# Three kept gates (0, 3 and 6) instead of two, two of them finished ahead of the Q blocks, a lower stock of conv work, and other segments at the end

## The chip, the cores and the metric

The kernel runs on the 8 cores of one Trainium2 chip, each with its own part of the tokens and without talk between them. Every core holds 1024 prompt tokens (with 32 more ahead of them, for the causal windows) and 64 sample tokens, and reads all weights. The metric is the device time of the slowest core, in microseconds (us); a kernel's time is the median of its runs.

## What is computed

One layer of a decoder with three head groups, then a final RMSNorm:

```python
h = rmsnorm(x, norm_g)
u_a, gate_a, glu_val, glu_gate, gate_b, q, gate_c = split(h @ w_in)     # 76 blocks of 128 columns
o_a = pool_mix(u_a, windows 2/4/8/16, w_pool) * silu(gate_a)            # head group A: 12 blocks
a   = glu_val * sigmoid(glu_gate)
o_b = (silu(layernorm(depthwise_conv31(a))) @ w_pw) * silu(gate_b)      # head group B: 12 blocks
o_c = cross_attention(q, mem_k, mem_v) * silu(gate_c)                   # head group C: 8 blocks, 4 heads
y   = rmsnorm(x + concat(o_a, o_b, o_c) @ w_out, final_norm_g)          # 32 blocks of 128 columns
```

For the prompt, mem_k and mem_v come from rmsnorm(mem_prompt) and two more matrices; for the samples they are read from a cache. States of the pooling and of the conv are also written out.

## The kernel before, in words

All activations lie transposed: channels on the partitions, the core's tokens along the columns (W = 1088, or NT = 1120 with the halo). A *block* is 128 output channels; a matmul unit is 256 KB of bf16 weights, eight k chunks of 128, and four units make a block of the input projection. Weights come through a ring of nine tiles, filled from GpSimd's queue in the order of use (`fill`, L364).

**Start.** While x is loaded, partial sums of some blocks are formed over the k chunks that are there (`SETS`, L439); those of two gates of head group A cover three of their four units and wait in `HGA`. Then `second_halves` (L768) finishes blocks: V 1, Q 0, Q 1 and, last, the two gates with `ga_spill(0)` and `ga_spill(1)` (L1065), which join the last unit, multiply by 1/rms (`RB`), take the silu and write the gate to DRAM. Their tiles are then used again by the memory's norm: `MQ` takes the squares of the memory (`mem_group`, L830), four times a square on ScalarE and a sum on VectorE, until `mem_hilo` writes `PBT` and TensorE can sum it (`mem_sum`). Memory K and V follow, as steps that `slip` puts between the units of other blocks (16 units each for K and V, twice).

**Middle.** The loop at L1166 sets the order of blocks by hand-made costs (`S.t`, `S.when`): a gate and a V block of head group B (`gg_block`, `v_block`) are issued when `backlog() < TH` (the conv work that waits for VectorE, in us) and when `others` has given at least `PACE` = 1.7 blocks for each pair before; else the next block of `others` goes (Q, gates of C, gates of B, some of which are spilled to DRAM through the tile `XG`). Every V block gives VectorE one depthwise conv (39 pieces), whose pieces are put between its other work (`pump`). `v_mult(j)` needs the tile EA[j % 2], so conv j - 2 must be done (`flush_conv`). After the last conv the LayerNorm is applied (L1134, L1135, silu L1131), and twelve pointwise blocks follow (`pw_block`), while spilled gates come back.

**Head group A.** Four groups: three u blocks each, with running sums on VectorE, the load of w_pool, then three gate blocks (`ga_block`) with a small product (`mix`) for each. Gates 0 and 1 come from DRAM.

**End.** 26 blocks of w_out for all columns (L1396); columns from T2 on (the last two of five segments) are parked in DRAM as partial results. Then the last six blocks run segment by segment (`SEG`): 6 x 32 matmuls a segment, the sum of squares, 1/rms, scaling of all 32 blocks on VectorE and GpSimd, stores on SP's queue. Parked blocks are reloaded into an area that an earlier segment has left (`AREA`, `reload`, L1536). `LP` holds the last six blocks of a segment, `xq_load` fetches their x on ScalarE's queue.

Of the kernel before, what the change touches and what calls it, by code (L numbers as in the profile page):

```python
# [16 lines left out]
KC = 32  # L17
NT = 1120
W = 1088
NP_ = 1024  # L20
EPS = 1e-6
NRING = 9
UNITS_AT_ONCE = 2
PACE = 1.7
UNIT_US = 1.85
SLACK = 1.8
TH = 90.0
POOLW = (2, 4, 8, 16)
# [3 lines left out]

SEG = ((0, 176), (176, 432), (432, 688), (688, 920), (920, W))
AREA = (0, 1, 2, 1, 0)
KEPT = [[0, 1, 2, 3], [4, 5, 6, 7], [8, 9, 10, 11], [12, 13, 14, 15, 16, 17], [18, 19, 20, 21], [22, 23, 24, 25]]
# [139 lines left out]
def build_program(loads=None):  # L175
# [34 lines left out]
    with contextlib.ExitStack() as st:  # L210
# [217 lines left out]
        def esa_load(j, after=()):  # L428
# [339 lines left out]
        def second_halves():  # L768

            z, zb = proj(BLK_V + 1, 32, 2)  # L770
            ev, _, evb = esa(1)
            dve(lambda e: e.tensor_tensor(out=EA[1][:, 0:1056], in0=EA[1][:, 0:1056], in1=z[:, 0:1056], op=ALU.add), 1056,
                r=[EAb[1], zb], w=[EAb[1]])
            dve(lambda e: e.tensor_tensor(out=ev[:, :, 30:34], in0=STs[:, 0:64].rearrange("p (s r) -> p s r", s=16),
                                          in1=z[:, 1056:NT].rearrange("p (s r) -> p s r", s=16), op=ALU.add), 64,
                r=[STsb, zb], wa=[evb])
            gate_mult(1)
            gate_mult(0)
            gate_sig(1)
            gate_sig(0)  # L780
            z, zb = proj(BLK_Q, 0, 2)
            gate_mult(1)
            q_out(0, z, zb)
            v_mult(1, None, None)
            gate_mult(0)
            v_mult(0, None, None)

            push_sample(0)
            push_sample(1)
            push_prompt(0)  # L790
            push_prompt(1)
            q_scale(0)
            z, zb = proj(BLK_Q + 1, 0, 2)
            q_out(1, z, zb)
            assert conv_done[0] < 0
            q_scale(1)
            given.add(("q", 0))
            for i in range(2):

                ga_spill(i)  # L800
                for k, v in HGA[i][1][0].r.items():
                    S._put(MQb.r, k, v)

# [258 lines left out]

        NGA = 2

        def ga_spill(i):  # L1065
            if i < 2:
                t, tb = rest(BLK_GA + i, HGA[i], 3)
                gate(t, tb[0], t, *tb)
            else:
                z, zb = proj(BLK_GA + i, 0)  # L1070
                t, tb = XG, KSTb
                gate(z, zb, t, *tb)
            S.dma("sp", lambda e: e.dma_start(out=gsp_d[26 - i], in_=t), r=tb, w=[GSPA[i]], kb=544)

        def gb_spill(i):
# [122 lines left out]
        for dj in range(12):  # L1198
            pw_block(dj)
            if dj < 5:  # L1200
                g, gb = GB[dj]
                S.dma("sp", lambda e: e.dma_start(out=g[:, 0:W], in_=gsp_d[27 + dj]), r=[GSP[dj]], w=[gb], sembuf=gb, kb=544)
            if dj in (7, 9):

                i = (dj - 7) // 2
                g, gb = GB[2 * i]
                S.dma("sp", lambda e: e.dma_start(out=g[:, 0:W], in_=gsp_d[26 - i]), r=[GSPA[i]], w=[gb], sembuf=gb, kb=544)

# [63 lines left out]
        def ga_block(j):  # L1272
            if j < 2:
                return
            if j < NGA:
                drain()
                g, gb = gates_a[j % 2]
                S.dma("sp", lambda e: e.dma_start(out=g[:, 0:W], in_=gsp_d[26 - j]), r=[GSPA[j]], w=[gb], sembuf=gb, kb=544)
# [159 lines left out]
        LPb = [[[like(p[2], "LP") for _ in range(3 - i)] for p in l] for i, l in enumerate(LP)]  # L1438
        assert 3 * N[0] + T3 <= W and all(3 * N[i] <= W for i in (2, 4)) and all(2 * N[i] <= 512 for i in (1, 3)) and HTX + 512 <= KC * NT // 2
        assert all(N[i] <= N[AREA[i]] for i in (3, 4))  # L1440
        for k in range(2):
            for b in LPb[0][k]:
                for key, v in ST[k][1].r.items():
                    S._put(b.r, key, v)
# [51 lines left out]
        def seg_sum(si):  # L1496
# [17 lines left out]
            for gi, g in enumerate(KEPT[0:NQ]):  # L1514
                ap, bs = area(gi, si), AB[gi][AREA[si]]
# [178 lines left out]
```

How the kernel before makes its waits and increments, by code:

```python
    def _wait(self, eng, key, val):  # L71
        if self.known[eng].get(key, 0) >= val:
            return
        if key == "pe":
            assert val <= self.cnt[key], "wait for a TensorE count that nothing raises yet"
        self.known[eng][key] = val
        self.h[eng].wait_ge(self.sems[key], val)
# [43 lines left out]
    def op(self, eng, fn, r=(), w=(), wa=(), inc=True, cost=0.1):  # L121
        ww = tuple(w) + tuple(wa)
        self.deps(eng, r, ww)
        end = self.when(eng, r, ww) + cost
        self.t[eng] = end
        for b in r:
            b.tr = max(b.tr, end + 0.1)
        for b in ww:
            b.tw = end + 0.1
            b.we = eng
        sem = self._sem(eng)
        ins = fn(self.h[eng])
        if inc:
            self.cnt[eng] += 1
            ins.then_inc(sem, 1)
            val = self.cnt[eng]
        else:
            assert eng == "pe"
            val = self.cnt[eng] + 1
        self._mark(eng, val, r, w, wa)
# [1 line left out]
    def dma(self, eng, fn, r=(), w=(), wa=(), sembuf=None, kb=None, beside=()):  # L142
# [7 lines left out]
            for b in ww:  # L150
                b.tw = self.tq + 1.0
                b.we = None
        sb = sembuf or (w[0] if w else r[0])
        if sb.dsem is None:
            sb.dsem = {}
        kind = "sw" if eng == "pool" else "hw"
        key = sb.dsem.setdefault(kind, ("dma", sb.name, id(sb), kind))
        sem = self._sem(key)
        self.cnt[key] += 16
        fn(self.h[eng]).then_inc(sem, 16)
        self._mark(key, self.cnt[key], r, w, tuple(wa) + tuple(beside))
```

## Time and profile before

| | us |
|---|---|
| median of 3 runs | 1841.94 (1841.41 to 1940.04) |
| the profiled execution | 1841.41 |
| its span on the slowest core, core 3 | 1840.3 |
| spans of the other cores | 1833.5 to 1839.4 |
| TensorE busy | 1790.8 (97%) |
| VectorE busy | 1057.7 (57%) |
| ScalarE, GpSimd busy | 375.9, 358.6 |

"Busy" of an engine is the time in which at least one of its instructions runs; matmuls overlap, so the mean of one is longer than the distance to the next. In the views, PE is TensorE, DVE VectorE, ACT ScalarE, POOL GpSimd, SP the queue of SyncE; `out<-in` are the program's tiles and L the line of the kernel. "[1.41 <-DVE Y L1566]" says that the engine stood idle for 1.41 us before the instruction, and what ended that. The granted clock is the share of TensorE's full clock that the chip let through: 1.00 is 2.4 GHz, 0.50 is 1.2 GHz.

### The profile page before, as it was taken

How to read it: one execution, taken by the hardware profiler on the slowest of the kernel's cores; microseconds unless marked ns; L12 is line 12 of the kernel's file. 1: busy time of each engine (PE TensorE's matmuls, PEld its weight loads, DVE VectorE, ACT ScalarE, POOL GpSimd, SP SyncE). 2: the span in 40 equal slices, each digit the busy share in tenths (PEclk: the TensorE clock that was granted, in tenths of full speed). 3: DMA queues.
4: the chain of work that ended last, by engine and by line, in shares of the span. 5: the costliest groups of instructions: out<-in, count | busy, mean ns of one | idle time of the engine just before them, and what ended most of it. 6: DMA issues, size and time to landing. Idle time of an engine off the chain costs nothing.

```text
span 1840.3 us, 31577 instructions; the slowest of 8 cores (1833.5 to 1840.3 us)
## 1 busy us (share of the span) xinstructions
PE 1790.8 (97%) x12286; PEld 927.3 (50%) x12286; DVE 1057.7 (57%) x1173; ACT 375.9 (20%) x599; POOL 358.6 (19%) x644
## 2 busy tenths in 40 slices
PE   6999999999999999999999999999999999999995
PEld 3444445555444555555444444444444444444695
DVE  3577997999899999998731332324311111212266
ACT  4534213112110211311410000000012222222211
POOL 2211221222222122212111111111111111111034
PEclk9999999999999999999999999999999999999998
DMA  9988788877999687777467656555657888766589
GB/s 237 245 187 178 110 131 129 139 110 115 136 167 151 103 117 124 117 108 112 66 125 112 95 80 85 76 85 79 107 98 136 140 142 138 140 121 127 92 244 312
DMA packets 126147, 244.57 MB, mean 133 GB/s; under 512 B 17072, under 2 KB 34736, under 8 KB 123440
## 3 DMA queue, kind: packets, MB, share of 16 engines
q0 software_dynamic: 87840, 168.79, 62.2%
q1 hardware_dynamic: 18864, 58.50, 10.1%
q10 hardware_dynamic: 19296, 15.26, 2.9%
q8 instruction: 99, 1.62, 0.4%
q14 instruction: 48, 0.39, 0.1%
HBM read 360.56 MB, written 34.63 MB: 215 GB/s over the span
## 4 chain that ended last, share of the span: by engine, by line
PE 88%; DMA 4%; issue 3%; DVE 3%; ACT 1%; POOL 0%; ACTq 0%; DVEq 0%; POOLq 0%; SPq 0%
PE Z L312 82%; PE PM L312 6%; DMA CC<-xT 2%; DMA ring<-w_in 1%; DVE KEEP L832 1%; DMA mkN<-KEEP 0%; DMA yT<-CC 0%; DMA KV<-w_pool 0%; ACT CC L546 0%; DVE CC L420 0%; POOL HT L1519 0%; PE PM L941 0%; ACT CC L831 0%; DVE CC L808 0%; DMA yT<-QS 0%
## 5 line engine op out<-in xcount | busy, mean ns | idle before, releaser
L312 PE MATMUL Z<-HT,ring 128*128 128x512 bf16 (+3 forms) x7184 | 1147.2, 319 | 21.2 <-DMA ring<-w_in 16.2
L312 PEld LDWEIGHTS Z<-HT,ring 128*128 128x128 bf16 x7184 | 555.3, 98 | 589.0 <-issue 29.7
L312 PE MATMUL Z<-CC,ring 128*128 128x512 bf16 (+5 forms) x3288 | 484.9, 311 | 0.2 <-DVE KEEP L970 0.2
L312 PEld LDWEIGHTS Z<-CC,ring 128*128 128x128 bf16 x3288 | 250.6, 98 | 233.1 <-issue 0.4
L373 POOL DMA_DIRECT2D ring<-w_in x304 | 161.9, 534 | 671.9 <-PE Z L312 387.9
L706 DVE SCALAR_TENSOR_TENSOR CC<-EA,CS,CC 128x1024 f32<-128x1024 f32 x180 | 230.0, 1278 | 0.0
L710 DVE SCALAR_TENSOR_TENSOR Y<-EA,CS,Y 128x1024 f32<-128x1024 f32 x168 | 214.7, 1278 | 0.0
L1409 DVE TENSOR_TENSOR HT<-Z,EA 128x256 f32<-128x256 f32 (+1 forms) x54 | 18.1, 391 | 199.4 <-PE Z L312 199.4
L373 POOL DMA_DIRECT2D ring<-w_out x113 | 59.6, 528 | 353.4 <-PE Z L312 334.0
L971 ACT ACTIVATE KEEP<-KEEP 128x1088 f32<-128x1088 f32 x21 | 23.3, 1111 | 215.4 <-DVE KEEP L970 215.3
L1239 DVE TENSOR_TENSOR EA<-Z,KEEP 128x1040 f32<-128x1040 f32 x12 | 14.9, 1242 | 87.6 <-PE Z L312 87.6
L312 PE MATMUL PM<-ring,CC 128*128 128x512 bf16 x256 | 59.7, 379 | 2.3 <-ACT KV L890 2.3
L1411 ACT ACTIVATE SG<-HT 128x256 f32<-128x256 f32 (+1 forms) x51 | 20.1, 395 | 188.4 <-DVE HT L1409 185.1
L1409 DVE TENSOR_TENSOR KEEP<-Z,EA 128x256 f32<-128x256 f32 (+1 forms) x24 | 8.0, 391 | 87.4 <-PE Z L312 87.4
L971 ACT ACTIVATE SG<-SG 128x1088 f32<-128x1088 f32 x6 | 6.7, 1111 | 252.1 <-DVE SG L970 252.1
L1414 DVE TENSOR_TENSOR SS<-SS,SG 128x1088 f32<-128x1088 f32 x25 | 32.3, 1292 | 26.7 <-ACT SG L1411 26.7
L1519 POOL TENSOR_TENSOR HT<-HT,SS 128x512 f32<-128x512 f32 (+3 forms) x30 | 33.4, 1145 | 69.5 <-DVE SS L1513 69.5
L970 DVE TENSOR_TENSOR KEEP<-Z,KEEP 128x1088 f32<-128x1088 f32 x20 | 25.7, 1287 | 33.3 <-PE Z L312 30.5
L1295 DVE SCALAR_TENSOR_TENSOR CC<-PM,CS,SG 128x512 bf16<-128x512 f32 (+1 forms) x18 | 10.7, 595 | 56.1 <-PE PM L312 55.4
L312 PEld LDWEIGHTS PM<-ring,CC 128*128 128x128 bf16 x256 | 23.4, 98 | 29.5 <-issue 2.6
L420 DVE TENSOR_TENSOR CC<-CC 128x2240 f32<-128x2240 f32 x15 | 37.3, 2486 | 0.2 <-DVE CC L420 0.2
L734 ACT ACT_TABLE_LOAD x9 | 11.5, 1283 | 119.4 <-DVE KEEP L733 88.5
(234 smaller groups left out, 1218.6 us busy)
## 6 DMA issues: line engine op xcount, KB each, us to landing
ring<-w_in POOLq DMA_DIRECT2D x304, 256.0 KB, 5.7
ring<-w_out POOLq DMA_DIRECT2D x113, 256.0 KB, 4.2
CC<-xT POOLq DMA_DIRECT2D x14, 1120.0 KB, 15.9
EA<-xT SPq DMA_DIRECT2D x26, 544.0 KB, 6.0
ring<-w_mem_k POOLq DMA_DIRECT2D x32, 256.0 KB, 6.7
ring<-w_mem_v POOLq DMA_DIRECT2D x32, 256.0 KB, 6.5
ring<-ckT POOLq DMA_DIRECT2D x32, 256.0 KB, 5.1
ring<-cvP POOLq DMA_DIRECT2D x32, 256.0 KB, 5.0
```

The source lines that it names most:

```text
L312: S.op("pe", lambda e: e.matmul(out, lhsT=lhsT, rhs=rhs, start=start, stop=stop, skip_group_check=skip), r=r, w=w, inc=inc, cost=max(0.026 ...
L373: S.dma("pool", lambda e: e.dma_start(out=RING[s][:, 0:n], in_=src), r=after, w=[RINGb[s]])
L420: dve(lambda e: e.tensor_tensor(out=ACC, in0=ACC, in1=SQ2[a % 2], op=ALU.add), 2240, r=[ACCb, SQ2b[a % 2]], w=[ACCb])
L706: piece(lambda e, k=k: e.scalar_tensor_tensor(out=YB[j][:, 0:NP_], in0=EA[b][:, 2 + k:2 + k + NP_], scalar=col(wc + k), in1=YB[j][:, 0:NP_ ...
L710: piece(lambda e, k=k: e.scalar_tensor_tensor(out=Y1[:, 0:NP_], in0=EA[b][:, 2 + k:2 + k + NP_], scalar=col(wc + k), in1=Y1[:, 0:NP_], op0 ...
L832: piece(lambda e: e.tensor_reduce(out=MA[:, g, :], in_=MQ.rearrange("p (k n) -> p n k", k=8), axis=AX.X, op=ALU.add), 3300, r=[MQb], wa=[M ...
L970: dve(lambda e: e.tensor_tensor(out=g[:, 0:W], in0=z[:, 0:W], in1=RB[:, 32:NT], op=ALU.mult), W, r=[zb, RBb], w=gb)
L971: act(lambda e: e.activation(out=g[:, 0:W], in_=g[:, 0:W], func=AF.Silu), W, r=gb, w=gb, tab="silu")
L1409: dve(lambda e: e.tensor_tensor(out=yv, in0=z[:, c0:c1], in1=xr[:, c0:c1], op=ALU.add), c1 - c0, r=[zb, xrb], w=[yb])
L1411: act(lambda e: e.activation(out=sq[:, c0:c1], in_=yv, func=AF.Square), c1 - c0, r=[yb], **({"wa": [sqb]} if i else {"w": [sqb]}))
L1414: dve(lambda e: e.tensor_tensor(out=SY[:], in0=SY[:], in1=SQo[:, 0:W], op=ALU.add), W, r=[SYb, SQob], w=[SYb])
L1519: S.op("pool", lambda e: e.tensor_tensor(out=yv, in0=yv, in1=over(SY[:, c0:c1], 2), op=ALU.mult), r=[SYs[si], b], w=[b], cost=0.3 + n * 0. ...
```

## The change

- **Which gates.** Of head group A, gates 0, 3 and 6 go through DRAM (before: 0 and 1). Gates 0 and 3 have three units done at the start; gate 6 is a whole block of `others`, after the gates of C. `ga_block` computes the other nine. Gate 0 is reloaded during the pointwise blocks, gates 3 and 6 after the first u block of groups 1 and 2.
- **When.** In `second_halves` the two gates are finished ahead of the Q halves: the first behind the sigmoids, the second when the first conv pieces have been queued. `ga_early` also carries the planned reading time of the spilled tiles over to `MQ`.
- **Stock.** `TH` 90 to 62.
- **Segments.** Widths 176, 256, 256, 232, 168 to 224, 256, 224, 224, 160. The parked columns become 384 (before 400). Segment 3 uses the area of segment 0 and segment 4 that of segment 1 (before the other way round). The reload of segment 3 goes behind the stores of segment 0, that of segment 4 in three pairs between the stores of segment 2 (before: of 4 behind 0, of 3 behind 1). The last six blocks' tiles no longer overlap the staging tiles.

```diff
+NGA = 3
-TH = 90.0
+TH = 62
-SEG = ((0, 176), (176, 432), (432, 688), (688, 920), (920, W))
-AREA = (0, 1, 2, 1, 0)
+SEG = ((0, 224), (224, 480), (480, 704), (704, 928), (928, W))
-                (((BLK_GA, NSEG), (BLK_GA + 1, NSEG)), 0, 12),
+                (((BLK_GA, NSEG), (BLK_GA + 3, NSEG)), 0, 12),
 def second_halves():
             gate_sig(1)
             gate_sig(0)
-            z, zb = proj(BLK_Q, 0, 2)
+            ga_early(0)
             gate_mult(1)
-            q_out(0, z, zb)
             v_mult(1, None, None)
             gate_mult(0)
             v_mult(0, None, None)
...
             push_prompt(0)
             push_prompt(1)
+            ga_early(1)
+            z, zb = proj(BLK_Q, 0, 2)
+            q_out(0, z, zb)
             q_scale(0)
             z, zb = proj(BLK_Q + 1, 0, 2)
             q_out(1, z, zb)
...
-            for i in range(2):
-                ga_spill(i)
-                for k, v in HGA[i][1][0].r.items():
-                    S._put(MQb.r, k, v)
+        def ga_early(i):
+            ga_spill(i)
+            b = HGA[i][1][0]
+            for k, v in b.r.items():
+                S._put(MQb.r, k, v)
+            MQb.tr = max(MQb.tr, b.tr)
...
-        NGA = 2
         def ga_spill(i):
             if i < 2:
-                t, tb = rest(BLK_GA + i, HGA[i], 3)
+                t, tb = rest(BLK_GA + 3 * i, HGA[i], 3)
...
+        def ga_back(i):
+            g, gb = GB[2 * (i % 2)]
+            S.dma("sp", lambda e: e.dma_start(out=g[:, 0:W], in_=gsp_d[26 - i]), r=[GSPA[i]], w=[gb], sembuf=gb, kb=544)
...
-            if dj in (7, 9):
+            if dj == 7:
+                ga_back(0)
...
         def ga_block(j):
-            if j < 2:
-                return
...
+            if j in (0, 3, 6)[0:NGA]:
                 return
...
                 u_block(3 * g + i)
+                if i == 0 and 0 < g < NGA:
+                    ga_back(g)
...
-            if final and si < 2:
-                reload(4 - si, (3, 0, 4, 1, 5, 2))
+            if si == 0 and final:
+                reload(3, (3, 0, 4, 1, 5, 2))
+            if si == 2:
+                reload(4, {NFULL + 3: (3, 0), KEPT[3][0]: (4, 1), KEPT[4][0]: (5, 2)}.get(dbs[0], ()))
```

## Rows read from the trace of the kernel before

**Rows 1.** The page, busy time of the engines: us, share of the span, instructions.

```profile
PE 1790.8 (97%) x12286; PEld 927.3 (50%) x12286; DVE 1057.7 (57%) x1173; ACT 375.9 (20%) x599; POOL 358.6 (19%) x644
```

**Rows 2.** Waits of TensorE, core 3: what for, us in total, times, longest.

```profile
PE Z L312 <- DVE ESA L749: 4.4, 1, 4.4
...
PE PM L312 <- DVE PBT L846: 2.5, 1, 2.5
PE PM L312 <- ACT KV L890: 2.3, 1, 2.3
PE Z L312 <- DVE Y L1566: 1.4, 1, 1.4
PE PM L312 <- DVE CC L1295: 0.9, 1, 0.9
PE PM L312 <- DMA KV<-w_pool: 0.7, 1, 0.7
```

**Rows 3.** Spans and mean granted clock of the two slowest cores.

```profile
core 2: 1839.4 us, clock 0.993
core 3: 1840.3 us, clock 0.993
```

**Rows 4.** Waits of TensorE, core 2.

```profile
PE Z L312 <- DVE ESA L749: 4.8, 1, 4.8
PE PM L312 <- DVE PBT L846: 3.1, 1, 3.1
...
PE PM L312 <- DVE SS L1571: 2.1, 1, 2.1
```

**Rows 5.** Timeline (start us, us, instruction), the matmul behind the last segment.

```profile
1822.18 0.52 PE L312 MATMUL PM<-SS,SG 128*128 128x168 f32 x2 [3.15 <-DVE SS L1571]
```

**Rows 6.** Stretch of the last stage: us, busy us of PE, PEld, DVE, ACT, POOL, clock, DMA share, GB/s.

```profile
1757.00:1823.00 66.00, 62.63 (x654) 59.00 (x652) 46.93 (x93) 10.47 (x27) 22.93 (x19) 1.00 0.98 296
```

**Rows 7.** Timeline of VectorE and ScalarE around the early gates.

```profile
132.07 1.32 DVE L596 TENSOR_TENSOR SG<-SG,KEEP 128x1120 f32<-128x1120 f32 x1
...
151.67 1.28 DVE L808 TENSOR_TENSOR CC<-CC,Z 128x1088 f32<-128x1088 f32 x1
...
162.43 1.91 ACT L831 ACTIVATE CC<-CC 128x2048 f32<-128x2048 f32 x1 [6.88 <-DMA yT<-CC]
```

**Rows 8.** Stretches after the waits for PBT and L749, columns as in rows 6.

```profile
195.20:198.60 3.40, 3.40 (x15) 1.40 (x15) 3.40 (x4) 2.31 (x2) 0.00 (x0) 0.53 0.31 57
235.90:242.70 6.80, 5.12 (x17) 2.02 (x18) 6.63 (x9) 3.13 (x4) 0.00 (x0) 0.50 0.96 160
```

**Rows 9.** Timeline of TensorE and VectorE, V block 2 and conv 0.

```profile
211.61 3.62 PE L312 MATMUL PM<-ring,CC 128*128 128x512 bf16 x16
...
225.89 3.85 PE L312 MATMUL Z<-HT,ring 128*128 128x512 bf16 x24
...
235.41 0.73 DVE L725 COPY SS<-CC 128x1088 f32<-128x1088 f32 x1
...
237.57 13.76 PE L312 MATMUL Z<-HT,ring 128*128 128x512 bf16 x72 [4.38 <-DVE ESA L749]
```

**Rows 10.** Timeline of TensorE, two blocks of segment 0.

```profile
1738.35 5.01 PE L312 MATMUL Z<-CC,HT 128*128 128x176 bf16 x64 [1.41 <-DVE Y L1566]
```

**Rows 11.** Timeline of VectorE, first block of segment 4.

```profile
1809.94 0.33 DVE L1566 TENSOR_TENSOR Y<-Z,EA 128x168 f32<-128x168 f32 x1 [2.43 <-DMA yT<-Y]
```

**Rows 12.** DMA issues, 1823 to 1840 us: number, KB each, median us to landing.

```profile
yT<-HT ACTq DMA_DIRECT2D x3, 336.0 KB, 6.7
```

**Rows 13.** DMA issues, 1750 to 1757.5 us.

```profile
yT<-Y SPq DMA_DIRECT2D x1, 264.0 KB, 3.1
```

**Rows 14.** Timeline from V block 11 to the first pointwise block.

```profile
794.71 0.22 DVE L749 TENSOR_TENSOR ESA<-Z,KEEP 128x64 f32<-128x64 f32 x1
...
929.76 1.29 ACT L1131 ACTIVATE CC<-CC,CS 128x1088 bf16<-128x1088 f32 x1 [1.30 <-DVE CC L1135]
931.26 28.95 PE L312 MATMUL Z<-CC,ring 128*128 128x512 bf16 x187
```

More of the change, by code:

```diff
@@ L1061, in build_program @@
         gsp_d = y_d.rearrange("(b p w) -> b p w", b=32, p=128)
-        NGA = 2
         def ga_spill(i):
             if i < 2:
-                t, tb = rest(BLK_GA + i, HGA[i], 3)
+                t, tb = rest(BLK_GA + 3 * i, HGA[i], 3)
                 gate(t, tb[0], t, *tb)
             else:
-                z, zb = proj(BLK_GA + i, 0)
+                z, zb = proj(BLK_GA + 3 * i, 0)
                 t, tb = XG, KSTb
@@ L1202, in build_program @@
                 S.dma("sp", lambda e: e.dma_start(out=g[:, 0:W], in_=gsp_d[27 + dj]), r=[GSP[dj]], w=[gb], sembuf=gb, kb=544)
-            if dj in (7, 9):
-                i = (dj - 7) // 2
-                g, gb = GB[2 * i]
-                S.dma("sp", lambda e: e.dma_start(out=g[:, 0:W], in_=gsp_d[26 - i]), r=[GSPA[i]], w=[gb], sembuf=gb, kb=544)
+            if dj == 7:
+                ga_back(0)
         EU = EA
@@ L1215, in build_program @@
         gates_a = [(SG[0], SGb[0]), (G[0], Gb[0])]
+        assert gates_a[0] == GB[0] and gates_a[1] == GB[2]
         SPB = [Buf("SPL%d" % i) for i in range(3)]
@@ L1272, in ga_block @@
         def ga_block(j):
-            if j < 2:
-                return
[L1275 to L1278, printed above, removed]
+            if j in (0, 3, 6)[0:NGA]:
                 return
@@ L1348, in area @@
             m = len(KEPT[gi])
-            o = at * T2 + m * SEG[AREA[si]][0]
+            o = at * T2 + m * SEG[si if si < 3 else si - 3][0]
             return base[:, o:o + m * N[si]]
@@ L1438, in build_program @@
         LPb = [[[like(p[2], "LP") for _ in range(3 - i)] for p in l] for i, l in enumerate(LP)]
[L1439 to L1444, printed above, removed]
+        assert all(3 * N[i] + T3 <= W for i in (0, 2, 4)) and all(2 * N[i] <= 512 for i in (1, 3)) and HTX + 512 <= KC * NT // 2
+        assert N[3] <= N[0] and N[4] <= N[1]
         def last_at(si, k):
             t, c0, _ = LP[si % 2][k]
-            if si in (2, 4):
-                c0 = 0
             return t[:, c0:c0 + len(LASTB[si % 2][k]) * N[si]]
@@ L1514, in seg_sum @@
             for gi, g in enumerate(KEPT[0:NQ]):
-                ap, bs = area(gi, si), AB[gi][AREA[si]]
+                ap, bs = area(gi, si), AB[gi][si % 3]
                 for i in range(0, len(g), 2):
@@ L1529, in seg_sum @@
             for gi, g in list(enumerate(KEPT))[NQ:]:
-                ap, bs = area(gi, si), AB[gi][AREA[si]]
+                ap, bs = area(gi, si), AB[gi][si % 3]
                 for i in range(0, len(g), 2):
@@ L1537, in reload @@
             for gi in gs:
-                bs, g = AB[gi][AREA[si]], KEPT[gi]
+                bs, g = AB[gi][si - 3], KEPT[gi]
                 S.dma("sp", lambda e: e.dma_start(out=area(gi, si), in_=far(si, g)), r=[ysp[db] for db in g], w=bs, sembuf=bs[0],
```

## The prediction

> **What bounds the kernel now.** I read the page first. TensorE is busy for 1790.8 us [rows 1] of core 3's 1840.3 [rows 3]: no other engine comes near it, so the change can win only the 49.5 us in which TensorE stands idle, and what it loses at half its clock. The change issues as many matmul columns as before, so I priced no work, only waits. The second view is therefore the list of TensorE's waits on core 3, the slowest [rows 2]; the third is the same list on core 2 [rows 4], which is only 0.9 us quicker [rows 3]: the time is that of the slowest core, so a gain counts only if both have it. The fourth is the timeline around each wait, to see what ends it; the fifth the granted clock behind it.
>
> Four places matter. (a) TensorE waits 2.5 us for PBT, the last result of the memory norm's chain. (b) It waits 4.4 us for L749, the second piece of the conv input of block 2. (c) It waits 2.3 us for the copy of transposed memory K (L890). (d) From its last main matmul, 1822.18 - 3.15 = 1819.03 us [rows 5], 21.3 us pass to the end at 1840.3, and there DMA decides: from 1757 us on its engines are busy 0.98 of the time at 296 GB/s [rows 6]. Small ones are 1.4 us at the first segment and 0.9 and 0.7 us in head group A [rows 2].
>
> The profiled execution took 1841.41 us, 1.1 us more than its span; the median of the runs is 1841.94. The sum is made against 1840.3 + 1.1.
>
> **The memory chain (early gates).** Before, the Q halves, four units of 3.7 us (24 matmuls, 3.85 us with the tail of the last [rows 9]), stand ahead of the two gate quarters. The second quarter is joined at 151.67 us; its spill goes out after that, and the square of the memory (L831), which writes over the spilled tiles, starts at 162.43, after 6.88 us of waiting for the spill to land [rows 7]. After the change VectorE's order decides: from the gate_mult at 132.07, which ends at 133.4 [rows 7], it has join, RB product, gate_mult, v_mult, gate_mult, v_mult, about 1.3 us each and 0.2 us for each v_mult's second piece, 8.2 us, so the second join comes near 142, 10 us earlier. If the spill takes as long and the chain too (162.43 to the matmuls at 195.2 [rows 7, 8], 32.8 us), the chain ends near 185.
> TensorE asks no earlier than before, so the wait can go. But its place is chosen by the kernel's own clock, which did not know that MQ waits for the spills; the added `MQb.tr` tells it. Bounds: nothing, if that clock is again short, and 2.5 us plus the clock: the 3.4 us after it were granted 0.53 [rows 8], so 3.4 x 0.47 = 1.6 are lost, 4.1 together. I take 3.6, nearer the upper end, because the late link itself is both moved and told. The moved instructions cost nothing: the same units and the same gates. The second Q half starts two units before 151.6, near 144.2, and asks for the Z that the second join reads until about 143.3: a microsecond of cover. If that is gone, TensorE waits for one or two conv pieces, 1.3 to 2.5 us. On SP's queue the two spills stand behind memT loads already issued, and before loads of later stages.
>
> **Less stock (TH 90 to 62).** Block 2's gate and V blocks are issued when fewer than TH us of conv work wait. One conv is 45 us by the costs in the code, so 90 is two whole convs: block 2 starts with conv 0 hardly begun. Its V product is complete at 211.61, where two memory units start; only the three units of the next block follow until TensorE waits at 233.2. VectorE can take the product only when conv 0 is out of EA[0]: L725, its last piece, starts at 235.41, and L749 releases TensorE at 237.57 [rows 9]. With 62, 28 us of pieces must be gone first, and two more blocks of `others` (3 and 4 units of 3.7 us, and about seven memory units of 3.62 / 2 = 1.8 [rows 9], 38 us) come before block 2. V 2 is then done near 211.6 + 38 = 249 us, 13 us after conv 0. Bounds: nothing, and all of the wait with its clock: 5.12 us of busy time at 0.50 [rows 8] cost 2.6, so 4.4 + 2.6 = 7.0. I take 6.9, all of it: 13 us are a margin.
> What is late next? Block 3 follows at once (the pace asks for 3.4 others, 4 are issued). Its V is done some 44 us later, near 293; conv 1, about 50 us after conv 0, near 286: enough. From block 4 on the pace of 1.7 others a pair holds the pairs back, and the change leaves it.
>
> **The third gate, and the K copy.** One gate block moves from head group A to `others`: 4 units each way, nothing in sum. Its spill uses XG, as the memory K and V results do, and that sharing makes wait (c): a spilled gate waits until mkN has landed, and L890 stands behind its silu on ScalarE. Whether they meet depends on where memory K ends, and this moves by one to three units. Bounds: 2.3 us gained, or as much lost at a new meeting; as one meeting is there to lose and one spill more to meet, I take 1.1. The two reloads in head group A (544 KB, on SP behind a state load) have two u blocks, eight units or 30 us, to land; without that cover each would show what a spill's landing shows, 6.9 us [rows 7]. In groups 1 and 2 the first mix now comes soon after the w_pool load, as in group 0, where it cost 0.7: 0 to 1.4 us lost, I take 0.7. The 0.9 us between two mixes back to back goes, as a gate block now stands between them. Net 0.2.
>
> **The segments.** In segment 0 TensorE fills four banks before it waits for VectorE. A block of 176 columns takes (5.01 - 0.1) / 2 = 2.45 us [rows 10], by columns one of 224 takes 3.1: four of them last 2.6 us longer, against a wait of 1.4. Gain 1.4, and bound by that.
> The tail: core 3 waits 3.15 us for L1571 [rows 5], core 2 only 2.1 [rows 4]. The difference I put down to 2.43 us in which VectorE waits for an old store out of Y [rows 11]. After the change no reload stands in the queue ahead of that store (the second one goes behind segment 2's stores), so 1.0. The last segment is 8 columns narrower and the parked columns 16 fewer: (32 x 8 + 26 x 16) x 512 bytes = 0.34 MB, at 296 GB/s 1.1 us. The queue: stores of the tail land 6.7 us after their issue [rows 12], the first one out of Y in this stage after 3.1 [rows 13], so up to 3.6 us. Bounds of the tail: 0, and 1.0 + 3.6 = 4.6; I take 2.5, the 1.0 and 1.1 and a little of the queue.
> The rows show only that the stage is full. By the Trainium skill, DMA: Bandwidth & Descriptors, section "Issuing engines are not separate DMA queues", transfers started by different engines interleave on the same 16 engines; so a reload moved behind segment 2's stores takes time from the x loads and stores around it, late in the stage, and by that rule the tail would rather grow. The third rival prices this from rows.
>
> **Sum.** 3.6 + 6.9 + 1.1 + 0.2 + 1.4 + 2.5 = 15.7 us: 1840.3 - 15.7 + 1.1 = 1825.7. Core 2 has more of (a) and (b), 3.1 and 4.8 [rows 4], but no wait at the first segment and not the 1.0, so it may end a microsecond behind: **1827 us**.
>
> **Rivals.** *Everything goes* (0.08): all terms at their upper ends, 4.1 + 6.9 + 2.3 + 0.9 + 1.4 + 4.6 = 20.2, so 1821. *The early gates don't do what they say* (0.17): the memory sum is again placed too early, and (c) only moves: 3.6 + 1.1 less, about 1832. For it: 6.88 us of landing that the kernel's clock takes for about 3; against: the link moves by 10. *The reload fills the tail* (0.07): the last segment's reload, 26 x 160 x 512 bytes = 2.1 MB, takes 7.2 us at 296 GB/s. If all of it still stands ahead of the tail's stores, the 2.5 is lost and 7.2 added: 1837. Against: it is issued about 15 us before the last matmul. *The stock runs dry* (0.04, the other side): V 11's product is taken by 794.9, the last swish ends at 929.76 + 1.29 = 931.05, and the first pointwise block starts at 931.26 and needs that swish for its 34th matmul, 33 x 28.95 / 187 = 5.1 us later [rows 14]. So the slack is 5.3 us, and 14.8 more with one more block behind V 11. Each block that TH pulls ahead of V 11 takes 14.8 away: with three, TensorE waits 24 us and then runs slowly, 1852, slower than before; with two it is still faster. It decides from the third block on. Against: the pace, not TH, holds the late pairs.
>
> **How the numbers follow.** Forecast 0.64 (its own range 1822 to 1832). 1819 to 1835 takes in it, "everything goes" and "early gates don't", and leaves out the other two rivals and the edges of these. 2% is 37 us, about what a measurement of this kernel can tell from no change; all of TensorE's idle time is 49.5: faster 0.01, same 0.98, slower 0.01.
>
> **What would show it.** Right: no wait for L749, none for PBT over 1 us; L831 near 152 us; the clock at 1.00 from 190 to 250; no wait for L1566; a tail of about 19 us. Wrong: a wait on the pointwise blocks between 930 and 945 us (stock dry), waits for w_pool in groups 1 and 2 over 1 us, store landings over 8 us at the end.

## The result, and the profile after

The kernel after takes 1833.7 us (median) beside 1841.9 of the kernel before, a ratio of 0.995 (95% interval 0.993 to 0.997): 8.2 us faster. Beside the experiments it was run again: 1833.6 against 1841.8, 0.995 (0.994 to 0.997). Some executions in which cores of one or both dies show a lower mean clock (0.81 to 0.98) took longer, whatever the kernel, and are left out of the medians and means here, also one of the kernel before (1860.6 us) that the ratios of the first group of experiments still contain, so that these lie up to 0.001 lower than the medians beside them. The forecast was 1827 with a range of 1819 to 1835, within 2%. So the size is inside the range, but only a good half of the 15.7 us of the sum arrived. The profiled execution took 1833.69 us.

The spans and mean granted clocks, kernel after:

```profile
core 0: 1832.4 us, clock 0.994
...
core 2: 1827.9 us, clock 0.995
core 3: 1828.8 us, clock 0.995
core 4: 1822.1 us, clock 0.995
core 5: 1824.8 us, clock 0.996
```

Core 3, the slowest before, is 11.5 us shorter (1840.3 to 1828.8). But the slowest core is now core 0, which was the quickest before (1833.5) and has won 1.1 us. The mean of the eight spans went from 1837.1 to 1826.2, by 10.9; the time, that of the slowest core, by 7.7 in these two executions (1841.41 to 1833.69).

The page (busy us, share of the span, instructions) and TensorE's waits on core 3 (what for, us, times, longest), kernel after; the first wait is the start of the kernel:

```profile
PE 1788.2 (98%) x12286; PEld 929.2 (51%) x12286; DVE 1057.8 (58%) x1173; ACT 371.3 (20%) x595; POOL 359.7 (20%) x644
```

```profile
PE Z L312 <- DMA ring<-w_in: 15.5, 1, 15.5
PE PM L312 <- DVE SS L1571: 2.2, 1, 2.2
PE PM L946 <- ACT PBT L927: 1.2, 1, 1.2
PE PM L312 <- DVE CC L1012: 1.1, 2, 0.9
PE PM L891 <- ACT PBT L881: 1.1, 1, 1.1
PE PM L312 <- DMA KV<-w_pool: 1.1, 2, 0.5
```

Against [rows 2] the large waits have gone from this list: L749 (4.4), PBT (2.5), the copy of transposed memory K (2.3, L890 before, L895 after), the first segment (1.4), the one between two mixes (0.9). None of the eight cores has one of the first three left. Three new ones stand in their place: 1.2 us for the softmax of the samples at 368 us (L946), 1.1 for L1012 at 377, a product of head group C for which VectorE is behind, and 1.1 at 524 (L891), where TensorE transposes memory K and waits for its bf16 copy. That last one is wait (c) in another form. The copy out of PSUM (L878), which comes first, has itself waited for a spilled gate to leave the tile that both use:

```profile
521.28 0.69 ACT L878 ACTIVATE KEEP<-PM,RM 128x512 f32<-128x512 f32 x1 [8.93 <-DMA yT<-KEEP]
...
524.39 0.55 PE L891 MATMUL PM<-IDB,PBT 128*128 128x128 bf16 x7 [1.10 <-ACT PBT L881]
```

The clock after the former waits is full; the columns of a stretch are us, busy us of PE, PEld, DVE, ACT, POOL, clock, DMA share, GB/s:

```profile
190.00:250.00 60.00, 60.00 (x366) 29.15 (x365) 56.22 (x49) 11.32 (x13) 15.00 (x28) 1.00 0.86 130
```

The timeline of core 3 (start us, us, instruction) at the places of [rows 7, 9]:

```profile
141.65 1.28 DVE L813 TENSOR_TENSOR CC<-CC,Z 128x1088 f32<-128x1088 f32 x1
...
154.63 1.91 ACT L836 ACTIVATE CC<-CC 128x2048 f32<-128x2048 f32 x1 [9.10 <-DMA yT<-CC]
...
194.36 0.42 DVE L851 TENSOR_TENSOR PBT<-KV,PBT 128x256 bf16<-128x256 f32 x1 [0.59 <-ACT PBT L850]
...
199.20 0.24 PE L312 MATMUL PM<-ONES,PBT 128*128 128x1 bf16 x4
...
230.06 0.73 DVE L725 COPY SS<-CC 128x1088 f32<-128x1088 f32 x1
```

The second join comes at 141.65 (forecast: near 142), the square at 154.63 (near 152). Yet PBT is ready at 194.36 + 0.42 = 194.8, as before, not at 185: VectorE's order is fixed, and the pieces of conv 0 now stand between the steps of the chain. What moved is the asking: TensorE comes for PBT at 199.20, behind 13 units of `others`, where before it came behind six units of `others` and five of block 2. Block 2 itself stands behind five of the `others` in place of two.

The first matmul behind the last segment, on cores 0 and 3 of the kernel after, as in [rows 5]:

```profile
1810.88 0.51 PE L312 MATMUL PM<-SS,SG 128*128 128x160 f32 x2 [2.20 <-DVE SS L1571]
```

```profile
1809.15 0.51 PE L312 MATMUL PM<-SS,SG 128*128 128x160 f32 x2 [2.20 <-DVE SS L1571]
```

The wait for L1571 is 2.2 on all cores (before 3.15 on core 3, 3.0 on core 6, 2.1 on the others). Core 3's last main matmul ends at 1809.15 - 2.20 = 1806.95, 12.1 us earlier than before. The tail from there to the end is 21.8 us on core 3 (before 21.3), 23.7 on core 0, 19.0 on core 5; over the eight cores it runs from 18.0 to 23.7, mean 20.7 (before 20.2 to 22.6, mean 21.2). The stores of a long tail land later: the same two groups of DMA issues (number, KB each, median us from issue to landing) in the tail of core 3 and, in the second fence, of core 0:

```profile
yT<-KEEP SPq DMA_DIRECT2D x2, 448.0 KB, 8.2
...
yT<-Y SPq DMA_DIRECT2D x1, 240.0 KB, 11.1
```

```profile
yT<-KEEP SPq DMA_DIRECT2D x2, 448.0 KB, 11.0
...
yT<-Y SPq DMA_DIRECT2D x1, 240.0 KB, 12.9
```

### The profile page after: what moved, and what is told of

The parts are those of the page before. It is cut to its first block, busy times and chain, and to the rows that moved or that the text cites. A ratio compares the mean times of both kernels' runs of the same rounds, so it can differ in the third digit from the quotient of the medians.

```text
span 1832.4 us, 31561 instructions; the slowest of 8 cores (1822.1 to 1832.4 us)
## 1 busy us (share of the span) xinstructions
PE 1788.2 (98%) x12286; PEld 929.2 (51%) x12286; DVE 1057.8 (58%) x1173; ACT 371.3 (20%) x595; POOL 359.7 (20%) x644
## 4 chain that ended last, share of the span: by engine, by line
PE 92%; DMA 3%; issue 2%; DVE 1%; ACT 1%; POOL 0%; DVEq 0%; SPq 0%; ACTq 0%; POOLq 0%
PE Z L312 86%; PE PM L312 6%; DMA CC<-xT 1%; DMA yT<-KEEP 0%; DMA KV<-w_pool 0%; DMA ESA<-scT 0%; DVE Y L710 0%; POOL HT L1519 0%; DMA cssT<-ESA 0%; PE PM L946 0%; DVE Z L577 0%; DVE KEEP L975 0%; DVE CC L706 0%; ACT CC L544 0%; ACT KEEP L878 0%
## 5 line engine op out<-in xcount | busy, mean ns | idle before, releaser
L312 PE MATMUL Z<-CC,ring 128*128 128x512 bf16 (+4 forms) x3288 | 484.9, 311 | 0.2 <-DVE KEEP L975 0.2
L1412 DVE TENSOR_TENSOR HT<-Z,EA 128x224 f32<-128x224 f32 (+1 forms) x54 | 18.5, 396 | 199.1 <-PE Z L312 199.1
L1414 ACT ACTIVATE SG<-HT 128x224 f32<-128x224 f32 (+1 forms) x51 | 20.4, 400 | 188.3 <-DVE HT L1412 163.4
L1412 DVE TENSOR_TENSOR KEEP<-Z,EA 128x224 f32<-128x224 f32 (+1 forms) x24 | 8.2, 396 | 86.9 <-PE Z L312 86.9
L1519 POOL TENSOR_TENSOR HT<-HT,SS 128x448 f32<-128x448 f32 (+2 forms) x30 | 33.4, 1146 | 66.5 <-DVE SS L1513 66.5
L1296 DVE SCALAR_TENSOR_TENSOR CC<-PM,CS,KEEP 128x512 bf16<-128x512 f32 (+1 forms) x15 | 8.9, 595 | 47.3 <-PE PM L312 46.8
L312 PE MATMUL Z<-CC,HT 128*128 128x224 bf16 (+2 forms) x360 | 34.4, 256 | 0.0
```

What stands on the lines that cost most here:

```text
L312: S.op("pe", lambda e: e.matmul(out, lhsT=lhsT, rhs=rhs, start=start, stop=stop, skip_group_check=skip), r=r, w=w, inc=inc, cost=max(0.026 ...
L1296: dve(lambda e: e.scalar_tensor_tensor(out=CC[:, 2 * j, c0:c1], in0=m[i][:, 0:c1 - c0], scalar=col(C_PSC + j), in1=ga[:, c0:c1], op0=ALU.m ...
L1412: dve(lambda e: e.tensor_tensor(out=yv, in0=z[:, c0:c1], in1=xr[:, c0:c1], op=ALU.add), c1 - c0, r=[zb, xrb], w=[yb])
L1414: act(lambda e: e.activation(out=sq[:, c0:c1], in_=yv, func=AF.Square), c1 - c0, r=[yb], **({"wa": [sqb]} if i else {"w": [sqb]}))
```

## The experiments

Two theories were put to the test: the prediction's, in which each part of the change takes its own wait, and one read from the trace after, in which TH alone moves the askings, the early gates are doubled by it, and the segments win nothing. Each kernel ran beside the kernel before, in three groups, each on one chip. "Mean span" is worked out from the listed spans: the mean over the eight cores and the compared runs, less that of the kernel before beside it (1833.6, 1837.0 and 1837.3 for the three groups); its error is about half a microsecond. It shows a small effect better than the time, which is that of whichever core is last. The kernel after stands in the second group alone, so against a kernel of another group it is compared by two such differences, with a larger error. The expected times count from 1841.9 us; beside the first group the kernel before took 1837.6, so there the differences are what is to be compared.

| kernel | us | before beside it | ratio (95%) | mean span |
|---|---|---|---|---|
| before + early gates | 1831.4 | 1837.6 | 0.996 (0.993 to 0.998) | -6.2 |
| before + TH 62 | 1836.5 | 1837.6 | 0.998 (0.996 to 1.001) | -1.6 |
| before + segments | 1837.2 | 1837.6 | 0.999 (0.997 to 1.001) | -0.2 |
| before + third gate | 1840.8 | 1842.2 | 1.000 (0.999 to 1.001) | -1.0 |
| after | 1833.6 | 1841.8 | 0.995 (0.994 to 0.997) | -10.5 |
| after, late gates | 1834.4 | 1842.2 | 0.995 (0.994 to 0.997) | -8.8 |
| after, TH 90 | 1836.2 | 1841.8 | 0.997 (0.996 to 0.998) | -6.3 |
| after, two gates | 1839.1 | 1841.8 | 0.999 (0.998 to 1.000) | -3.3 |
| after, old segments | 1828.9 | 1837.6 | 0.994 (0.992 to 0.997) | -9.8 |
| after, reload earlier | 1831.5 | 1841.8 | 0.995 (0.993 to 0.996) | -9.6 |
| after, old segments, TH 70 | 1828.8 | 1842.2 | 0.993 (0.992 to 0.995) | -12.0 |
| after, no reload | 1829.1 | 1842.2 | 0.993 (0.991 to 0.994) | -12.5 |

### Early gates alone

```diff
-            z, zb = proj(BLK_Q, 0, 2)
+            ga_early(0)
             gate_mult(1)
-            q_out(0, z, zb)
...
             push_prompt(1)
+            ga_early(1)
+            z, zb = proj(BLK_Q, 0, 2)
+            q_out(0, z, zb)
...
-            for i in range(2):
...
-                ga_spill(i)
...
```

> Alone: the two gates (0 and 1) finished ahead of the Q halves, with the reading time told to MQ; TH 90, the old segments and two kept gates stay. Theory of the prediction: the chain to PBT comes 10 us earlier, so TensorE's wait for PBT (2.5 us on core 3 of the kernel before) goes and with it the slow clock after it, 3.6 us in all; the wait for L749 (4.4) stays; about 1838. Rival: the kernel after shows PBT ready at the same time as before (194.8 against 194.6 us), and its wait gone only because TensorE asks later; then the wait for PBT stays here at 1 to 2.5 us, and the time is 1840 to 1842.

0.996, 6.2 us by the medians: more than either theory gave. Waits of core 3, and the two instructions that decide them:

```profile
PE PM L312 <- ACT KV L895: 2.5, 1, 2.5
PE Z L312 <- DVE ESA L749: 1.7, 1, 1.7
```

```profile
188.06 0.43 DVE L851 TENSOR_TENSOR PBT<-KV,PBT 128x256 bf16<-128x256 f32 x1 [0.60 <-ACT PBT L850]
...
227.73 0.73 DVE L725 COPY SS<-CC 128x1088 f32<-128x1088 f32 x1
```

Here the step of the prediction is seen as it was meant: the last step of the chain starts 6.5 us earlier (at 194.55 before), not the ten forecast, and no wait for PBT is left on any core. And the last piece of conv 0 starts 7.7 us earlier too (235.41 in [rows 9]), as VectorE has the chain behind it sooner; so 2.7 of the 4.4 us for L749 go as well. That second gain was not in the sum.

### TH 62 alone

```diff
-TH = 90.0
+TH = 62
```

> Alone: TH 62 in place of 90. Theory of the prediction: the wait for L749 goes with its slow clock, 6.9 us; the wait for PBT stays at 2.5 (it was to be taken by the early gates); about 1835. Rival: TH alone puts more of the other blocks ahead of block 2, so TensorE also asks for PBT later; both waits go, 6.9 and 3.6, and the time is 1831 to 1833, below or level with the kernel after (1833.8).

Both waits are gone from core 3, as the rival said, and yet the time is the same within the interval. Much of the gain was given back at the pointwise blocks. Core 3, last swish and TensorE:

```profile
925.74 1.29 ACT L1131 ACTIVATE CC<-CC,CS 128x1088 bf16<-128x1088 f32 x1 [1.31 <-DVE CC L1135]
```

```profile
917.68 4.92 PE L312 MATMUL Z<-CC,ring 128*128 128x512 bf16 x30
924.58 0.62 PE L312 MATMUL Z<-CC,ring 128*128 128x512 bf16 x3 [1.98 <-ACT CC L1131]
927.17 13.02 PE L312 MATMUL Z<-CC,ring 128*128 128x512 bf16 x67 [1.98 <-ACT CC L1131]
```

The first pointwise block starts at 917.68, 13.6 us earlier than before [rows 14], and the swishes are not there: two waits of 1.98, and from 925 to 930 us a granted clock of 0.55. This is the prediction's fourth rival, the dry stock. It did come, with TH alone.

### Segments alone

```diff
-SEG = ((0, 176), (176, 432), (432, 688), (688, 920), (920, W))
-AREA = (0, 1, 2, 1, 0)
+SEG = ((0, 224), (224, 480), (480, 704), (704, 928), (928, W))
...
-            if final and si < 2:
-                reload(4 - si, (3, 0, 4, 1, 5, 2))
+            if si == 0 and final:
+                reload(3, (3, 0, 4, 1, 5, 2))
+            if si == 2:
+                reload(4, {NFULL + 3: (3, 0), KEPT[3][0]: (4, 1), KEPT[4][0]: (5, 2)}.get(dbs[0], ()))
...
```

> Alone: the widths 224, 256, 224, 224, 160, the exchanged areas and the places of the two reloads. Theory of the prediction: no wait for the first segment (1.4 on core 3), the wait for L1571 from 3.15 to about 2, the tail from 21.3 to about 19; 2 to 4 us in all, about 1838. Rival: the tail of the kernel after is no shorter than before (19 to 24 us, with landings 8 to 13 us behind their issue on the cores 0 to 3), since the reload of segment 4 now stands between the stores of segment 2; then the 1.4 is won and lost again, 1841 to 1844, and the tail is 20 to 24 us.

No difference that can be measured. The wait at the first segment is gone and that for L1571 is 2.2, but the former was on core 3 alone of that size (0.3 and 0.5 on cores 2 and 7 of the kernel before, none on the others), and the tail is still 18.3 to 22.3 us, mean 19.9.

### After with the old segments

```diff
-SEG = ((0, 224), (224, 480), (480, 704), (704, 928), (928, W))
+SEG = ((0, 176), (176, 432), (432, 688), (688, 920), (920, W))
+AREA = (0, 1, 2, 1, 0)
...
-            if si == 0 and final:
-                reload(3, (3, 0, 4, 1, 5, 2))
-            if si == 2:
-                reload(4, {NFULL + 3: (3, 0), KEPT[3][0]: (4, 1), KEPT[4][0]: (5, 2)}.get(dbs[0], ()))
+            if final and si < 2:
+                reload(4 - si, (3, 0, 4, 1, 5, 2))
...
```

> The kernel after with the old segments (176, 256, 256, 232, 168), areas and places of the reloads; three gates, early gates and TH 62 stay. Theory of the prediction: 3.9 us slower than the kernel after, about 1838, with the wait for the first segment (1.4) and that for L1571 (3.15) back. Rival (the new segments cost in the tail what they win ahead of it): the same as the kernel after or faster, 1830 to 1834, with a tail of 20 to 22 us.

The rival: 0.994 against 0.995, and the mean span differs by 0.7. Neither of the two waits is back as it was: L1571 is waited for 2.1 us on all eight cores, the first segment at most 0.2. The tail is 18.8 to 20.6 us, mean 19.5. So the segments are worth 0.2 us alone and 0.7 as the last part added, which is no more than the error.

### After with TH 90

```diff
-TH = 62
+TH = 90.0
```

> The kernel after with TH 90 in place of 62. Theory of the prediction: the wait for L749 comes back in full with its slow clock, 6.9 us slower than the kernel after. Rival, from the early gates alone: they bring the end of conv 0 forward by 7.7 us (L725 at 227.73, before 235.41) and leave 1.7 us of that wait on core 3; then TH 62 is worth only 2 to 3 us here, and the pointwise blocks have more than 10 us in hand.

The waits of core 3:

```profile
PE Z L312 <- DVE ESA L749: 2.5, 1, 2.5
PE PM L312 <- ACT KV L895: 2.3, 1, 2.3
```

2.6 us slower by the medians, 4.2 by the mean span: nearer the rival, with one thing that neither theory had. The wait for the copy of memory K is back in its old form, with three gates kept, and the one at L891 is gone. So the form of wait (c) goes with TH.

### After with two gates

```diff
-NGA = 3
+NGA = 2
```

> The kernel after with two kept gates (0 and 3): gate 6 is computed in head group A, so one block (four units, 14.8 us) less stands ahead of the pointwise blocks; early gates, TH 62 and the segments stay. Theory 1 (the third gate is what keeps the stock from running dry): the first pointwise block starts near 921 us in place of 936 while the last swish ends near 928 to 931, so TensorE waits 1 to 4 us for swish between 921 and 935, and its clock falls after that: 2 to 6 us slower than the kernel after. Theory 2 (the early gates keep it from that, as they bring the convs forward): no such wait, and the time of the kernel after within 1 us.

Theory 1. Core 3's TensorE, and the stretch with its clock:

```profile
921.88 4.92 PE L312 MATMUL Z<-CC,ring 128*128 128x512 bf16 x30
928.78 0.66 PE L312 MATMUL Z<-CC,ring 128*128 128x512 bf16 x3 [1.98 <-ACT CC L1139]
931.37 13.93 PE L312 MATMUL Z<-CC,ring 128*128 128x512 bf16 x74 [1.94 <-ACT CC L1139]
```

```profile
929.00:935.80 6.80, 4.86 (x17) 1.76 (x16) 2.13 (x2) 1.30 (x1) 0.53 (x1) 0.52 0.24 37
```

The pointwise blocks start at 921.88 (936.19 after), wait 3.9 us and run at half clock behind it, 4.86 x 0.48 = 2.3 us: 6.2 together, measured 7.2 in the mean span and 5.5 in the medians. The prediction booked the third gate as "nothing in sum"; it is the cover of TH 62.

### After with the reload earlier

```diff
-            if si == 2:
-                reload(4, {NFULL + 3: (3, 0), KEPT[3][0]: (4, 1), KEPT[4][0]: (5, 2)}.get(dbs[0], ()))
+            if si == 1 and final:
+                reload(4, (3, 0, 4, 1, 5, 2))
```

> The kernel after with the reload of segment 4 issued as a whole behind the stores of segment 1, in place of three pairs between the stores of segment 2. Theory 1 (the reload stands in the queue ahead of the last stores and holds them back): landings of the tail come down from 8 to 13 us to 5 to 8, the tail from 20.7 us (mean of the cores) by 2 to 3, 1831. Theory 2 (the tail is as long as its own work and its own stores, whatever stands ahead): the tail and the time stay within 1 us of the kernel after.

No difference that these runs can tell from the kernel after: the four compared runs have a median 2.2 us lower, the mean span is 0.9 higher, and the intervals overlap. So theory 2 by the tail, whose mean is 20.0 us beside 20.7 and 20.1. But the profile shows both mechanisms, one against the other. Core 3, VectorE in the last segment, TensorE behind it, and the same stores as above:

```profile
1799.80 0.33 DVE L1566 TENSOR_TENSOR Y<-Z,EA 128x160 f32<-128x160 f32 x1 [3.14 <-DMA yT<-Y]
...
1811.73 0.87 PE L312 MATMUL PM<-SS,SG 128*128 128x160 f32 x2 [4.16 <-DVE SS L1571]
```

```profile
yT<-KEEP SPq DMA_DIRECT2D x2, 448.0 KB, 2.8
...
yT<-Y SPq DMA_DIRECT2D x1, 240.0 KB, 4.2
```

The landings come down from 8 to 11 us to 3 to 6, and in return VectorE waits for the old store out of Y, which now stands behind the reload, and the wait for L1571 is 2 us longer.

### After with late gates

```diff
-            ga_early(0)
+            z, zb = proj(BLK_Q, 0, 2)
             gate_mult(1)
+            q_out(0, z, zb)
...
-            ga_early(1)
-            z, zb = proj(BLK_Q, 0, 2)
-            q_out(0, z, zb)
...
+            for i in range(2):
...
+                ga_spill(i)
...
```

> The kernel after with the two gates finished behind the Q blocks again, as before; three gates (0, 3, 6), TH 62 and the new segments stay. Theory 1 (TH 62 moves TensorE's asking for PBT to 199 us, behind its 194.5, so the early gates cover a wait that is gone anyway): within 1 us of the kernel after. Theory 2 (the prediction: the early gates carry 3.6 us of their own): 3 to 4 us slower than the kernel after, with a wait for PBT of 1 to 3 us or a wait for swish between 921 and 940.

Theory 1 by the ratio, 0.995 as the kernel after; the mean span gives 1.7 us, and the waits say where some of it may be: cores 4 and 5 wait 0.6 us for PBT, and they and cores 0, 2 and 6 wait 0.8 for the memory's 1/rms (L855). On core 3 PBT is ready later than in the kernel before and isn't waited for:

```profile
196.41 0.42 DVE L846 TENSOR_TENSOR PBT<-KV,PBT 128x256 bf16<-128x256 f32 x1 [0.60 <-ACT PBT L845]
```

```profile
198.59 0.24 PE L312 MATMUL PM<-ONES,PBT 128*128 128x1 bf16 x4
```

### Third gate alone

```diff
+NGA = 3
...
-                (((BLK_GA, NSEG), (BLK_GA + 1, NSEG)), 0, 12),
+                (((BLK_GA, NSEG), (BLK_GA + 3, NSEG)), 0, 12),
...
```

> The kernel before with gates 0, 3 and 6 as the kept ones, gate 6 among the other blocks; the late gates, TH 90 and the old segments stay. Theory of the prediction: the copy of memory K (L890) no longer stands behind the spill of a gate, 0 to 2.3 us gained, about 1 us. Rival (the kernel after with TH 90 shows that wait still at 2.3 us, so that it goes with TH and not with the gates): the wait stays at 2 to 3 us and the time is that of the kernel before within 1 us; the third gate is worth something only where TH 62 lets the stock run dry.

The rival: no difference. The wait for the copy of memory K stays, 1.2 us on core 3, 3.8 on core 0.

### After with the old segments and TH 70

```diff
-TH = 62
+TH = 70
...
-SEG = ((0, 224), (224, 480), (480, 704), (704, 928), (928, W))
+SEG = ((0, 176), (176, 432), (432, 688), (688, 920), (920, W))
...
```

> The kernel after with the old segments and TH 70: block 2 goes behind four other blocks in place of five, block 5 behind seven in place of eight, block 6 behind nine in place of ten. Theory 1: no wait for L749 (block 2 is still 13 us or more behind conv 0), and the waits for the sample softmax at 368 and 377 us (0.5 to 3 us and 0.9 on the cores of the kernel after) go, as they do with TH 90: 1 to 3 us faster than the kernel after. Theory 2: the copy of memory K stands in the way at 521 us again, as with TH 90 (2 to 3 us): the same as the kernel after or slower by 1 to 2.

Each theory is half right. The waits at 368 and 377 us are gone, and L749 isn't waited for; in return core 3 waits 1.7 us for the copy of memory K and 0.4 for L1003, core 0 1.8 and 2.0. The ratio is 0.993 (0.992 to 0.995), the best of the complete kernels: 13.4 us below the kernel before beside it, where the kernel after is 8.1 below. The intervals of the two ratios just overlap, and the mean spans differ by 1.5, so I call it at least as fast as the kernel after; that it is faster is not shown.

### After without the reload of segment 4

```diff
-            if si == 2:
-                reload(4, {NFULL + 3: (3, 0), KEPT[3][0]: (4, 1), KEPT[4][0]: (5, 2)}.get(dbs[0], ()))
```

> The kernel after without the reload of segment 4: the 26 parked blocks of that segment are not read back (2.1 MB), the scaling takes what stands in the tiles. Theory 1 (from 60 us before the last main matmul on the DMA engines are full, and the end comes when all bytes are through): the tail shrinks from 20 us by 4 to 7, the time by as much. Theory 2 (the tail is the chain of its own work: sum of squares, scaling, stores and their landing): tail and time within 1 us of the kernel after. Leaves out part of the result.

Between the theories. Core 0, the 15 us ahead of the last main matmul's end and the tail, first of the kernel after, then without the reload:

```profile
1793.70:1808.70 15.00, 14.98 (x210) 14.78 (x208) 9.96 (x23) 2.46 (x7) 6.07 (x6) 1.00 1.04 344
1808.70:1832.40 23.70, 1.02 (x4) 0.59 (x4) 9.82 (x23) 0.96 (x3) 5.67 (x7) 0.58 0.84 293
```

```profile
1792.50:1807.50 15.00, 14.99 (x210) 14.78 (x208) 9.96 (x23) 2.46 (x7) 6.06 (x6) 1.00 0.73 226
1807.50:1825.80 18.30, 1.02 (x4) 0.59 (x4) 9.83 (x23) 0.96 (x3) 5.68 (x7) 0.62 0.81 307
```

With the DMA engines at 0.73 in place of 1.04 ahead of it, the tail is 17.5 to 18.6 us on all eight cores, mean 18.0; with the reload it is 18.0 to 23.7 and 18.0 to 24.8 in two executions, means 20.7 and 20.1. So about 18 us are what is left without the reload, and the reload adds 0 to 7, by core and run.

## Why the prediction was right, and where it was not

The two effects that the prediction priced highest came: the waits for PBT and for L749 are gone on all cores. What it had wrong is how (a) goes, what moves (c), the size of the tail, and new waits that the sum doesn't have. That the size is inside the range is in part luck. 1833.7 lies outside the forecast's own range of 1822 to 1832, in the part that was added for the rival "the early gates don't do what they say", and that rival didn't happen.

**The memory wait (a).** The effect came on all cores, the mechanism as put did not decide in the kernel after: the chain did not end near 185 but at 194.8. Alone, the early gates do what the step says, by 6.5 us in place of ten (188.1, no wait). Beside TH 62 the wait goes without them (PBT at 196.8, asked for at 198.59). The prediction moved only the chain and held that "TensorE asks no earlier than before"; it asks 6.5 us later (199.2; before, it got PBT at 195.2 [rows 8] after 2.5 us of waiting). Its own next step, TH, does that: in the profiles, core 3 comes for PBT between 191 and 193 us with TH 90 and between 197 and 200 with TH 62.

**The stock (b).** The 6.9 us came: the last piece of conv 0 started at 230.06. The margin was larger than reckoned, as three more blocks went ahead of block 2 and not two: its V product was complete at 260.4, where 249 was forecast. But the 6.9 are not TH's alone: the early gates take 2.7 of the 4.4 by themselves.

**The copy of memory K (c).** The 2.3 us for L890 went, and 1.1 came back at L891, so 1.2 are left; 1.1 were taken. The price is right, and the prediction's bound named the reason, "as much lost at a new meeting". But it is TH that moves the meeting, not the third gate, which alone leaves the wait as it is, and with TH 90 too. On core 3 with TH 90 the copy of the transposed memory stands behind a spilled gate's silu on ScalarE; in the kernel after a spilled gate is ahead of memory K's first copy, and this one waits 8.93 us for the gate's store.

**What TH brings in.** The failed term ahead of the tail is one that the sum does not have: asked what is late next, the prediction looked at V 3 alone. The rows behind the wait at 368 us are a chain of queues, core 3 of the kernel after:

```profile
343.78 0.26 DVE L693 TENSOR_SCALAR CC<-CC,CS 128x64 f32<-128x64 f32 x1
...
352.16 0.27 ACT L965 COPY STs<-PM 128x128 f32<-128x128 f32 x1 [12.30 <-PE PM L312]
352.48 0.34 ACTq L680 DMA_DIRECT2D cssT<-ESA  x1
...
359.81 0.34 SPq L430 DMA_DIRECT2D ESA<-scT  x1
364.72 0.23 DVE L749 TENSOR_TENSOR ESA<-Z,SG 128x64 f32<-128x64 f32 x1 [5.42 <-DMA ESA<-scT]
365.59 1.28 ACT L922 ACT_TABLE_LOAD   x1 [12.60 <-DVE SM L919]
```

The sample part of a conv is done at 344.0. Its store out of ESA stands on ScalarE's queue behind a copy that waits 12.3 us for TensorE, and goes out 8.4 us later; the load of the next state waits for that store, VectorE waits 5.42 us for the load, and behind VectorE's instruction stands the softmax of the samples, for which TensorE then waits. With the wait at 377, where VectorE takes the product (L1012) only behind pieces of a conv, it makes 2.3 us on core 3. In the profiles with TH 62 both are there on most cores, with three gates or two, early gates or late; with TH 70 or 90 no core has either.

**The sum ahead of the tail, core 3.** Gone are 2.5 + 1.6, 4.4 + 2.6, 2.3, 1.4 and 0.9, together 15.7; new are 1.2, 1.1, 1.1 and 0.4 more for w_pool, 3.8. The difference, 11.9, agrees with the 12.1 by which the last main matmul ends earlier. The prediction had 13.2 there. Its 0.7 us for w_pool in groups 1 and 2 were not lost: no core waits for w_pool there, only in group 0.

**The tail.** This is the term that was mis-sized outright: 2.5 us less were taken; core 3 shows 0.5 more, and the mean over the cores 0.5 less (1.1 in the second execution). Nor do the segments shorten it: the mean tail of the six profiles with the old segments is 19.5 to 21.2 us, of the six with the new ones and their reload 19.9 to 22.8. The 1.0 for L1571 came (2.2), on the two cores that had it to lose; some 0.2 MB fewer were moved on core 3 (26.9 MB in place of 27.1 from 90 us ahead of the last main matmul's end on); and still the end did not come nearer. "A little of the queue" had the wrong sign in this place: on core 3 the landings of the tail's stores went from 5 to 8 us to 8 to 11. The reload that no longer stands ahead of the store out of Y stands ahead of the last stores (landings of 8 to 13 us, "wrong" by the prediction's own list), and the experiment that puts it back ahead turns the one into the other at the same price. The Trainium skill, DMA: Bandwidth & Descriptors, section "Issuing engines are not separate DMA queues", says that transfers started by different engines interleave on the same 16 engines. The trace agrees as far as the stretch shows it: with these full (share 1.04) the stores landed later; but the mean tail did not grow, which the prediction drew from that rule, nor did it shrink by the 2.5. The third rival, "the reload fills the tail", had the right mechanism, and the price of 7.2 us was too high: without the reload the mean tail is 2.1 to 2.7 us shorter, on core 0, the worst, 5.4.

**Which core.** The sum was made for cores 3 and 2, the ones with the longest waits, with one microsecond for the other. Core 0 had little of (a) (0.4 us) and of (c) (0.9) to lose, got the new waits, two waits for w_pool of 1.02 and 1.12 us near 1056 and a fall of the clock to 0.56 for 3.4 us after them, and the longest tail. In the second profiled execution core 2 is the slowest, with a tail of 24.8 us. Taking the largest of eight spans gives back what the mean wins: before, the slowest core stood 3.4 us above the mean of the eight, averaged over the runs (1840.4 against 1837.0), after, 5.1 (1831.6 against 1826.5). Without the reload it is 2.6 (1827.4 against 1824.8), which points to the tail's scatter as the larger part of it; other parts are not ruled out.

**The stock runs dry.** The prediction gave this 0.04 and asked how many blocks TH pulls ahead of V 11. The place and the reckoning of the slack were right, and the mechanism is real: it takes much of the gain of TH 62 alone, and of the kernel after with two gates. In the kernel after it does not show, because the third gate puts the pointwise blocks at 936.19, some 10 us behind what they need. The prediction named that block's 14.8 us of slack and still booked the gate as "nothing in sum". The parts are not a sum: the worth of each, by mean span, alone and as the last one added, is 6.2 and 1.7 for the early gates, 1.6 and 4.2 for TH, 1.0 and 7.2 for the third gate, 0.2 and 0.7 for the segments.

## What to carry to other kernels

A wait has two ends, the one who is late and the one who asks: two edits that each cure it are worth it once, and an edit that puts work ahead of the asker takes that work from the cover of a later stage, so look there too. Where the DMA engines are full, as in this last stage, moving the reload only chose who waits for it, and leaving its bytes out was what shortened the end; so count bytes before order. And forecast the slowest of the cores, not the one that is slowest now: a gain in waits that this core alone has is gone at the next core.

## What was not expected of the hardware

The tail of one kernel on cores with the same work differs by 5.7 us in one execution (18.0 to 23.7), with the DMA engines at 1.04 just ahead of it on core 0, and by 1.1 (17.5 to 18.6) where 2.1 MB less are read ahead of it (0.73). And of waits of about the same size some cost the clock and some do not: on core 0 two waits of 1.02 and 1.12 us for w_pool, with 0.6 us of matmuls between them, were followed by 3.4 us at 0.56; on core 3 the single wait of 1.2 us at 368 us was followed by no fall (1.00 from 368 to 373). Nor does the longer wait lose more: in the second profiled execution core 4 waits 3.04 us at that place and keeps 1.00 (370 to 374), where in the kernel before 2.49 us of waiting for PBT were followed by 0.53 [rows 8]. What decides it is not shown. Core 0 of the kernel after:

```profile
1055.45 0.59 PE L312 MATMUL PM<-QS,KV 128*128 128x512 bf16 x2 [1.02 <-DMA KV<-w_pool]
1057.16 0.59 PE L312 MATMUL PM<-KEEP,KV 128*128 128x512 bf16 x2 [1.12 <-DMA KV<-w_pool]
```

```profile
1057.60:1061.00 3.40, 3.40 (x14) 1.46 (x13) 1.50 (x2) 0.00 (x0) 0.00 (x0) 0.56 0.61 111
```
